# Gated linear attention in a decoder trunk: sample states, norms and gates of a head moved among the next head's levels

## What is computed

```python
b = jnp.cumsum(ac, axis=1)
decay = jnp.exp(jnp.where(causal, b[:, :, None] - b[:, None, :], -jnp.inf))
scores = jnp.einsum('bihd,bjhd,bijhd->bhij', qc, kc, decay)
o = einsum(scores, vc) + einsum(qc * exp(b), h)
h_new = jnp.exp(b_last)[..., None] * h + einsum(kc * exp(b_last - b), vc)
...
o = rms_norm(o, a_g_onorm).astype(h.dtype) * jax.nn.silu(g)
h = h + jnp.concatenate([tok, mem_o], axis=-1) @ w_out
```

## Time and profile before

| | us |
|---|---|
| median of 3 runs | 2760.83 |
| profiled execution, its own time | 2758.99 |
| its span, first to last instruction | 2757.1 |
| TensorE matmul busy | 2579.6 (94%) |
| DVE busy | 1133.7 (41%) |
| GpSimd busy | 937.1 (34%) |
| ScalarE busy | 504.7 (18%) |
| mean granted TensorE clock | 0.952 of 2.4 GHz |

### The profile page before, as it was taken

The page is one execution under the profiler, slowest core; times in us unless marked ns, Lnnn a source line. Parts: engine busy times, 40 slices in busy tenths (PEclk is TensorE's granted clock), DMA queues, the critical chain, the costliest instruction groups (busy, mean ns, idle before and its releaser), DMA issues.

```text
span 2757.1 us, 40482 instructions
## 1 busy us (share of the span) xinstructions
PE 2579.6 (94%) x16393; PEld 2449.5 (89%) x16393; DVE 1133.7 (41%) x1691; ACT 504.7 (18%) x970; POOL 937.1 (34%) x457
## 2 busy tenths in 40 slices
PE   3899987888999999999999889999799999999999
PEld 3899976766989999999999778777799999999998
DVE  6421217643453333333333756532753333333333
ACT  2332114313120000000001334112310000000000
POOL 6333344310333333333334343300223333333332
PEclk9999998876999999999999899979899999999999
DMA  4111130030211111111111220330001111111112
GB/s 174 55 39 34 52 138 2 3 124 31 100 34 51 47 46 46 46 46 46 46 46 46 100 85 24 100 136 1 31 31 46 46 46 46 46 46 46 46 46 77
DMA packets 39409, 154.88 MB, mean 56 GB/s; under 512 B 3841, under 2 KB 10497, under 8 KB 36881
## 3 DMA queue, kind: packets, MB, share of 16 engines
q1 hardware_dynamic: 26928, 98.05, 11.2%
q10 hardware_dynamic: 12384, 55.43, 5.2%
HBM read 135.14 MB, written 18.33 MB: 56 GB/s over the span
## 4 chain that ended last, share of the span: by engine, by line
PE 74%; DVE 3%; issue 1%; ACT 1%; DVEq 0%; ACTq 0%
PE bank L491 21%; PE bank L493 21%; PE bank L492 21%; PE bank L1055 1%; PE bank L1030 1%; PE bank L1050 1%; PE bank L759 1%; PE bank L1027 1%; PE bank L918 1%; PE bank L767 1%; PE bank L746 1%; PE bank L745 1%; PE bank L879 0%; PE bank L515 0%; PE bank L1026 0%
## 5 line engine op out<-in xcount | busy, mean ns | idle before, releaser
L491 PE MATMUL bank<-x_hi,w_hi 128*128 128x344 f32 (+1 forms) x3304 | 1075.1, 325 | 40.0 <-DVE x_lo L1564 12.5
L492 PE MATMUL bank<-x_lo,w_hi 128*128 128x344 f32 (+1 forms) x3304 | 1060.4, 321 | 0.0
L493 PE MATMUL bank<-x_hi,w_lo 128*128 128x344 f32 (+1 forms) x3304 | 1059.8, 321 | 0.0
L417 POOL TENSOR_TENSOR w_hi<-w_raw,zero 128x1024 fp32r<-128x1024 f32 x187 | 360.7, 1929 | 1615.7 <-PE bank L493 1615.4
L491 PEld LDWEIGHTS bank<-x_hi,w_hi 128*128 128x128 f32 x3304 | 628.2, 190 | 56.1 <-issue 53.3
L492 PEld LDWEIGHTS bank<-x_lo,w_hi 128*128 128x128 f32 x3304 | 628.0, 190 | 1.8 <-issue 0.7
L493 PEld LDWEIGHTS bank<-x_hi,w_lo 128*128 128x128 f32 x3304 | 627.9, 190 | 0.0
L419 POOL TENSOR_TENSOR w_lo<-w_raw,w_hi 128x1024 fp32r<-128x1024 f32 x187 | 462.1, 2471 | 14.7
L1841 DVE TENSOR_TENSOR hid<-sil,bank 128x344 f32<-128x344 f32 x132 | 67.7, 513 | 781.7 <-PE bank L493 743.8
L491 PE MATMUL bank<-hid_hi,w_hi 128*128 128x344 f32 x1056 | 339.9, 322 | 0.0
L492 PE MATMUL bank<-hid_lo,w_hi 128*128 128x344 f32 x1056 | 337.7, 320 | 0.0
(11 more groups left out here) (287 smaller groups left out, 1933.2 us busy)
## 6 DMA issues: line engine op xcount, KB each, us to landing
w_raw<-in_w SPq DMA_DIRECT2D x187, 512.0 KB, 3.4
h<-in_x ACTq DMA_DIRECT2D x3, 1376.0 KB, 15.3
h_spill<-h ACTq DMA_DIRECT2D x1, 4128.0 KB, 11.8
h<-h_spill ACTq DMA_DIRECT2D x1, 4128.0 KB, 12.4
out_y<-h ACTq DMA_DIRECT2D x3, 1376.0 KB, 5.7
g_spill<-ring ACTq DMA_DIRECT2D x6, 516.0 KB, 2.6
g_a<-g_spill ACTq DMA_DIRECT2D x1, 3096.0 KB, 17.1
h<-in_x ACTq DMA_DIRECT2D x1, 3096.0 KB, 10.1
```

What stands on the lines that cost most here:

```text
L417: nc.gpsimd.tensor_tensor(w_hi[:, s], w_raw[:, s], zero[:].broadcast_to([P, 1024]), ALU.add).then_inc(s_whi, 1)
L491: pe.matmul(out, wh, xh, start=(i == 0), stop=False)
L492: pe.matmul(out, wh, xl, start=False, stop=False)
L493: mm = pe.matmul(out, wl, xh, start=False, stop=(i == n - 1))
```

## The change

The norms, gates and sample states of head hh - 1 are put among the levels of head hh; of the work behind the last head only head 3's is left.

- `dec` has three buffers; GpSimd may be one level further ahead. `keep` of level l - 2, not l - 1, stands behind `decayed` of level l.
- The gate tiles go through Silu when they are evacuated from PSUM; the table of logarithm and exponential is loaded again ahead of the DMA of the level masks.
- `outs_kept` squares the outputs and scales them with the norm's gain: 8 operations in place of 4. `out_sums`, `out_logs` and `out_rstds` of a head come at levels 3 to 5 of the next (both halves at level 3 in head 3), the product with the root (`out_gated`) on DVE at level 7 (6 in head 3), and the product with the gate on GpSimd behind level 8, for heads 0 to 2. For head 3 both are on DVE.
- Sample tokens: keys and values are laid out on 32 partitions for each token of a group of four (`sample_values`, `sample_keys` in head 0), so that 8 updates use four row groups, and 8 outputs four column groups. Updates of head r are made at level 6 of head r + 1, states at levels 7 and 8 (4 operations each), outputs at level 8; those of heads 2 and 3 at levels 4 to 7 of head 3. ScalarE norms them (`sample_kept`).
- The sample states go through a ring of two, which lies, with the sample operands, in the memory of `w_hi` and `w_lo`: SyncE loads and writes them and the gates, between weight units 33 and 34. GpSimd splits units 31 and 32 only when the sample work is done.

```diff
+            if hh >= 1:
+                half = slice(HD * ((hh - 1) % 2), HD * ((hh - 1) % 2) + HD)
+                prompt = slice(0, SEQ)
+                pool.wait_ge(s_gland, 32 * hh)
+                pool.wait_ge(s_onm, 3 * hh - 1)
+                x = o_a[:, hh - 1, prompt]
+                nc.gpsimd.tensor_tensor(x, x, g_rows[0][:, 0, prompt], ALU.mult).then_inc(s_onm, 1)
+                pool.wait_ge(s_onm, 3 * hh)
+                x = o_a[half, 4 + (hh - 1) // 2, prompt]
+                nc.gpsimd.tensor_tensor(x, x, g_rows[0][half, 1, prompt], ALU.mult).then_inc(s_y, 1)
+                pool.wait_ge(s_y, hh)
+            pool.wait_ge(s_sn, 8 * H)
+            pool.wait_ge(s_sout, 16 * H)
+            pool.wait_ge(s_so, H)
+            pool.wait_ge(s_sx, SX_OUTS)
+            for u in range(U_AOUT, U_AOUT + 2):
+                split_unit(u)
...
-                    if n >= 2:
-                        pool.wait_ge(s_mu, n - 1)
+                    if n >= 3:
+                        pool.wait_ge(s_mu, n - 2)
...
+                for b in range(2):
+                    cols = slice(512 * b, 512 * b + 512)
+                    nc.scalar.activation(o_sq[:, 0, cols], banks[4 + b][:], ACT.Square)
+                    nc.scalar.activation(o_sq[half, 1, cols], banks[6 + b][half], ACT.Square).then_inc(s_osq, 1)
+                    nc.scalar.activation(o_a[:, hh, cols], banks[4 + b][:], ACT.Copy, scale=gain[:, G_ON:G_ON + 1]).then_inc(s_oe, 1)
+                    nc.scalar.activation(o_a[half, 4 + hh // 2, cols], banks[6 + b][half], ACT.Copy, scale=gain[half, G_ON + 1:G_ON + 2]).then_inc(s_oe, 1)
...
-                    if 1 <= l:
-                        keep(hh, l - 1)
+                    h0, l0 = divmod(NSTEP * hh + l - 2, NSTEP)
+                    if h0 >= 0 and l0 <= NLEV:
+                        keep(h0, l0)
                     if l == 1 and hh >= 1:
                         states(hh - 1)
+                    if 1 <= hh < H - 1:
+                        if l == 7:
+                            out_gated(hh - 1, slice(0, SEQ))
+                            sample_states(hh - 1, 0)
+                        if l == 8:
+                            sample_states(hh - 1, 1)
```

More of the change, by code:

```diff
@@ new lines, in sample_updates @@
+            def sample_updates(r):
+                pe.wait_ge(s_sxk, SK_KEYS)
+                pe.wait_ge(s_oln, 2 * min(r + 1, H - 1))
+                pe.wait_ge(s_zb, 3 * min(r + 3, H))
+                if r == H - 1:
+                    pe.wait_ge(s_sst, 4 * r)
+                for m in range(2):
+                    for j in range(4):
+                        rows = slice(32 * j, 32 * j + 32)
+                        mm = pe.matmul(banks[4 + j][:, m * DV:(m + 1) * DV], k_one[rows, r, m], v_one[rows, r * DV:(r + 1) * DV], start=True, stop=True)
+                mm.then_inc(s_su, 1)
@@ L711, in _, with sample_outs @@
+            def sample_outs(r):
+                pe.wait_ge(s_sn, 8 * (r + 1))
+                pe.wait_ge(s_prep, SP_QUERIES)
+                for m in range(2):
+                    for j in range(4):
+                        mm = pe.matmul(banks[4][32 * j:32 * j + 32, 0:DV], q_one[:, r, m, 32 * j:32 * j + 32], st_ring[:, r % 2, 4 * m + j],
+                                       start=(m == 0), stop=(m == 1))
+                mm.then_inc(s_so, 1)
             pe.wait_ge(s_ev, 8 + 3 * NA_IN)
@@ L1306, in _ @@
             act.wait_ge(s_cp, NBLK * H)
[L1307 removed]
+            act.wait_ge(s_sn, 8 * H)
             act.wait_ge(s_gst, 16 * H)
[L1309 to L1322 removed]
@@ new lines, in _ @@
+            keep(H - 1, NLEV)
+            states(H - 1)
+            dve.wait_ge(s_sx, SX_OUTS)
+            dve.wait_ge(s_gsmp, 16)
+            for rows, bk, g0 in ((slice(0, 4), banks[0], G_ON), (slice(4, 6), banks[1], G_ON + 1)):
+                n = rows.stop - rows.start
+                for j in range(4):
+                    op = nc.vector.scalar_tensor_tensor(out=o_a[:, rows, SEQ + j:T:4], in0=bk[:, 0:n * P].rearrange("p (n m) -> p n m", n=n)[:, :, 32 * j:32 * j + 2],
+                                                        scalar=gain[:, g0:g0 + 1], in1=g_smp[:, rows, j::4], op0=ALU.mult, op1=ALU.mult)
@@ L1797, in add_residual @@
+            for c in range(NCH):
+                if c < 2:
+                    out_gated(H - 1, slice(512 * c, 512 * c + 512))
+                dve.wait_ge(s_chi, NCH + c + 1)
+                mix_lo(slice(3, 6, 2), chunk(c), o_a[:, 3:6:2, chunk(c)])
             def add_residual(order, mm0, u0, per_unit, n0):
```

486 lines of the change are left out of this document (291 added, 195 removed).

## The result

The changed kernel takes 2746.18 us, the median of 4 runs (2745.98 to 2747.52), beside 2763.22 us for the kernel before in the same session (2757.32 to 2765.73). The ratio is 0.9942, 95% interval 0.9924 to 0.9961: faster by more than the 0.3% that counts here. Its profiled execution has a span of 2744.4 us, 12.7 us under that of before.

A forecast was written before the change was run, and what follows sets the result against it. Levels bound by hand-offs between engines, then a serial tail; the rest, bound by TensorE's products, unchanged. Levels +71 less tail 81.7 gives -10.7: about 2748 us profiled, 2750.5 by the median, range 2725 to 2770.

The forecast's parts named there:

- The tail gives back 81.7: Behind head 3's outputs (end O): first product at O+14.5, not O+86.0 (71.5 us); next three groups 13.4, not 23.6 (10.2).
- The levels grow by 71: Work added among the four heads' levels lengthens them: 20 us to head 1's level 3, 32 for two middle heads, 19 head 3.
- The start, +1.3 by the table load: Before the first level: a 1.28 us table load ahead of the level masks' DMA delays DVE's first work by 1.3 us.
- Level 3, +3.1 per head: Level 3, three heads: ScalarE's decay waits behind outputs kept (1.95 to 3.9 us), TensorE for one keep more (1.1).
- The scans, a gap of almost 8: DVE's log decay (1.2 us) and scans (4.2) precede the keep of level 4; TensorE idles almost 8 us before level 6.
- The gates of GpSimd hold the next head up: GpSimd's two gate products, 2.4 us each, stand ahead of the next head's level 0 exponents, plus about 1 us contention.
- The third buffer is worth nothing: Third decay buffer: GpSimd may run one level further ahead, hiding the outputs' wait on GpSimd, which ends on ScalarE anyway.
- The sample update, 1.4 us (0 to 2.6): Sample update on 32-row groups, shown by no row: taken as 1.4 us, between nothing and the old 8 matmuls' 2.6.
- (a): Rival: the levels take in the additions more cheaply; with half of the 71 hidden, -46, 2715 us. Chance 0.15.
- (b): Rival: longer TensorE gaps lower the clock in the levels and outputs, +20, 2770 us. Chance 0.2.
- (c): Rival: GpSimd-DVE contention, levels grow 78 to 80, 2759 us; sign: two-operand DVE operations over 2 us during gates. Chance 0.2.
- (d): Rival: late splits of weight units 31 to 33 bind the tail; 10 us longer halves or removes the gain, 2755. Chance 0.05.

The follow-up runs named there:

- k4: Changed kernel with GpSimd's split of weight unit 33 held until DVE has gated the first half of head 3: 2744.31 us.
- k7: Changed kernel with GpSimd's set-up for the sample tokens (a copy and a clear) moved behind the exponents of level 1: 2747.51 us.
- k2: Changed kernel with two decay buffers instead of three: 2744.38 us.
- k3: Changed kernel with GpSimd's gates of heads 0 and 1 moved from behind level 8 to behind the next head's level 1 exponents: 2740.20 us.
- k8: Changed kernel with all keeps back in the old order (level l - 1) plus the edits of k3, k4, k5 and k7: 2725.96 us.
- k9: k8 plus sample states behind level 8's product, norm product and gates later, head 3's outputs kept and logarithms later: 2709.99 us.
- k5: Changed kernel with DVE's products of levels 0 and 1 of head 0 ahead of the mask cast, two clears and the memory query set-up: 2747.15 us.
- k6: Changed kernel with only the keep at level 6 put back ahead of the next head's log decays and scans: 2740.64 us.
- k11: k9 with GpSimd's wait and query operand clear, and ScalarE's sample key copies, moved behind head 1's first exponents and decay: 2709.01 us.

## Why the prediction was right, and where by luck

The forecast, 2750.5 us and faster with 0.5, lies 4.3 us above the result. (Its own sum, 10.7 us under the median of 2760.83, gives 2750.1; the 0.4 us between change nothing below.) By its own steps:

- **The tail gives back 81.7.** The outputs end at 654.5, and the first product is at O+14.1, predicted O+14.5. The next three groups take 13.1 us: DVE adds the residual of the third at 681.85, after a wait of 3.25 us for TensorE; predicted 13.4. So 71.9 + 10.5 = 82.4 us. Its parts were less good. ScalarE's eight activations took 5.3 us in place of 3.9. With the 4 us allowed for waits I had DVE free at O+7.5; it began to gate at 661.1 (O+6.6), but its two norm products lost 2.8 us to the weight split behind that point, as k4 showed, and not ahead of it.
- **The levels grow by 71.** They grew by 72.0 (O at 654.5 against 582.5): level 3 of head 1 came 18.1 us later (forecast 20), the two middle heads took 34.2 us more (32), head 3 to its outputs 19.7 us more (19). So the walk is right head by head; inside a head it is luck in part, as the next points show. Sum: -10.4 us, forecast -10.7; the span fell by 12.7. The other 2.3 us lie behind the second chunk's first product, in code that the change leaves alone, and were not followed.
- **The start, +1.3 by the table load: the wrong cause.** It was +1.8 us. In the trace of the changed kernel the table load starts at 391.85 and the DMA of the masks is issued at 391.88, beside it; before it was issued at 392.22. The masks came no later. The cast did, 2.65 us instead of 0.69. With a third buffer GpSimd goes on to the exponents of level 2 (396.49 to 398.75 us), which fall on the cast; before, it stopped at 395.45, having filled both buffers. k7, where the cast begins just ahead of them, and k2, which has no third buffer, have the cast at 0.69 and 0.73 us.
- **Level 3, +3.1 per head.** The place is right. TensorE waits 5.91 us ahead of 602.99 in head 3, and in heads 1 and 2 for the outputs kept ahead of the gate products (L693, 5.8 us in two). Its size, 3.1 us, no run takes apart.
- **The scans, a gap of almost 8.** The gap is 4.2 to 5.6 us: this term of the walk was too large by 2 us or more. I took 4.21 us for the scans from a row in which GpSimd worked beside them. The step missed the other half: the level behind the gap at 1.2 GHz, 1.7 us. In head 1 that is 5.6 + 1.7 = 7.3 us, so two errors cancelled and the sum came out.
- **The gates of GpSimd hold the next head up.** Right, and priced by k3: 3.0 us for each of two heads.
- **The third buffer is worth nothing.** Right by the median of k2; but not neutral, since it shortens the scans and lengthens the cast.
- **The sample update, 1.4 us (0 to 2.6).** 0.9 to 1.7 us for eight matmuls, by the clock: 0.93 at 563.24 us in the changed kernel (clock 1.00), 1.66 at 602.31 us in k8.

Of the rivals, (a), that the additions are taken in more cheaply, did not happen in the order of the change. But the runs show that it was open. From the end of the input products to the outputs of head 3 the kernel before takes 191.2 us (391.3 to 582.5), the changed one 263.6 (390.9 to 654.5), k9 228.9 (392.0 to 620.9): with the same work, about half of the growth is gone. That half was the order of the lists, not the work added. I had priced the moved keep as 1.1 us at level 3 and as a gap at level 6. As the place of all keeps it cost 18 us. The right question at that step would have been what TensorE waits for next, and whether anything else stands ahead of it in DVE's list.

(b), the clock, did not take hold in the outputs (9.4 us from 645.1), but it did in the levels: seven groups of 16 matmuls in the rows above take 3.57 to 3.79 us. The Trainium skill (TensorE: Matmul & The Clock Gate, The HAM clock gate) has the clock fall after idling; the trace agrees at each of the eight waits of 4.24 to 6.74 us in the levels, with 3.50 to 3.79 us for the group behind. (c), contention, is real where the two engines meet (k2, k3, k4, k7). Around the gates it was what the walk allowed: GpSimd's two products took 5.7 us (501.41 to 507.07; forecast 4.8 and 1 for contention), DVE's pair behind them 2.9 (forecast 2.5). Its sign showed in one place, the product of level 8 in head 3 at 632.04, 2.54 us beside the gates instead of 1.21. The meeting on the scans is gone in the changed kernel. The Trainium skill (SBUF — State Buffer, SBUF: two separate sides) has one of the two engines stand still while the other's instruction runs; this case agrees: the cast of 0.69 us took 2.65, from 396.66 to 399.31 us, until GpSimd's exponents had ended at 398.75. (d) did not happen: the splits ended at 664.8, O+10.3, as predicted (O+10), and the first product was released by x_lo.

## What to carry to other kernels

When work is put among the steps of a loop that hands data from engine to engine, look first at what TensorE waits for, and put that ahead of everything else in each engine's list; here the order of the same instructions was worth 36 us, more than twice what the change brought. A single such move can give nothing (k5, k7) or less than half of what was expected of it (k6), because the wait reappears at the next step: judge by the trace of the place behind, and move all of a kind. And before a duration is taken from a row, look at what GpSimd or DVE did in that time.

## What the runs showed of the hardware

- DVE's eight scans of 128 columns take 2.63 us alone and 4.21 us with a GpSimd product of 128 x 1024 beside them, which goes from 1.90 to 2.82 us. In k2 that product ran beside DVE's log decays for 1.1 us and beside the scans for 1.7; the excess of scans and product, 2.5 us, is nearly the whole of that overlap.
- A cast of 128 x 1024 from f32 to bytes takes 0.69 us alone and 2.65 us beside GpSimd's exponents; a product of 128 x 512 takes 0.68 us alone and 2.83 beside GpSimd's gates (k3). Where the cast began first (k7), it kept its 0.69 us, and the exponents took 1.55 instead of 1.04.
- A ScalarE table load (1.28 us at 391.85) does not hold up a DMA that ScalarE's queue issues behind it (391.88).
- Behind each of eight TensorE waits of 4.24 to 6.74 us in the changed kernel a group of 16 matmuls took 3.50 to 3.79 us, against 2.05 at the full clock. Shorter waits went either way: 3.68 us behind 3.93 and 3.75 behind 2.96 us (kernel before, 474.68 and 482.19), 2.02 behind 2.51, 3.29 behind 1.46 (k11), mostly 2.02 to 2.05 behind less. So the cost of a wait is not proportional to its length.
- Eight sample updates on four groups of 32 rows (128 x 192 each) took 0.93 us at the full clock. In the kernel before, eight of them on 8 rows, one after another, took 5.45 us at the lower clock (630.01 us): an estimate from that row is 2.7 us at the full one.
